# A second feed-forward that begins with two plain chunks in place of four, and the order of ScalarE and VectorE up to there

## The reference

```python
x = x + 0.5 * swiglu_ffn(rms_norm(x, ffn1_norm), ffn1_w_in, ffn1_w_out)
...  # attention and a recurrent branch side by side, then x = x + [A, B] @ w_out_proj
x = x + 0.5 * swiglu_ffn(rms_norm(x, ffn2_norm), ffn2_w_in, ffn2_w_out)

def swiglu_ffn(h, w_in, w_out):          # w_in 1024 x 5632, w_out 2816 x 1024
    g, u = jnp.split(h @ w_in, 2, axis=-1)
    return (jax.nn.silu(g) * u) @ w_out
```

## Time and profile before

| | us |
|---|---|
| median of 3 runs | 896.06 (895.53 to 896.11) |
| the profiled execution | 896.09 |
| its span | 894.3 |
| TensorE busy | 885.5, 5458 matmuls |
| VectorE busy | 670.2 |
| ScalarE busy | 476.7 |
| GpSimd busy | 66.1 |
| mean granted clock of TensorE | 1.00 |

### The profile page before, as it was taken

How to read it: one execution, slowest core, us unless ns; L and a number is a source line. 1 busy time by engine, 2 the same in 40 slices (tenths; PEclk the granted TensorE clock), 3 DMA queues, 4 the chain that set the end, 5 groups by cost and what they waited for, 6 DMA issues and landing times.

```text
span 894.3 us, 14559 instructions
## 1 busy us (share of the span) xinstructions
PE 885.5 (99%) x5458; PEld 788.3 (88%) x5458; DVE 670.2 (75%) x1203; ACT 476.7 (53%) x811; POOL 66.1 (7%) x97
## 2 busy tenths in 40 slices
PE   8999999999999999999999999999999999999998
PEld 7899988999999888888886788899988899999886
DVE  6998864788887567876889787798854788887342
ACT  6766522467665244456657655476621567765120
POOL 0011100112110000000000000011100111210000
PEclk9999999999999999999999999999999999999999
DMA  7366533677775324322221021267633667775340
GB/s 245 127 147 173 146 118 106 166 196 181 183 179 149 107 85 150 101 88 94 95 95 48 1 95 51 99 158 184 158 106 117 165 169 200 178 183 152 106 129 35
DMA packets 26685, 117.70 MB, mean 132 GB/s; under 512 B 3216, under 2 KB 3344, under 8 KB 19344
## 3 DMA queue, kind: packets, MB, share of 16 engines
q1 hardware_dynamic: 16128, 88.32, 28.4%
q0 software_dynamic: 10512, 28.84, 17.6%
HBM read 86.74 MB, written 2.10 MB: 99 GB/s over the span
## 4 chain that ended last, share of the span: by engine, by line
PE 95%; DVE 3%; DMA 1%; ACT 1%; issue 0%; SPq 0%; DVEq 0%; ACTq 0%
PE bank L1482 31%; PE bank L1484 31%; PE bank L1483 30%; PE bank L1709 1%; PE bank L1732 1%; DMA raw<-w_in_dram 1%; DVE w_lo L904 0%; PE bank L1722 0%; DVE small L1403 0%; PE bank L1643 0%; DVE o L1450 0%; ACT probs L855 0%; SPq L418 0%; DVE a_s L1426 0%; DVE x L1393 0%
## 5 line engine op out<-in xcount | busy, mean ns | idle before, releaser
L1482 PE MATMUL bank<-t_hi,w_hi 128*128 128x256 f32 (+1 forms) x848 | 252.5, 298 | 0.6 <-DVE q_part L995 0.5
L1484 PE MATMUL bank<-t_hi,w_lo 128*128 128x256 f32 (+1 forms) x848 | 251.1, 296 | 0.0
L1483 PE MATMUL bank<-t_lo,w_hi 128*128 128x256 f32 (+1 forms) x848 | 250.9, 296 | 0.0
L1482 PEld LDWEIGHTS bank<-t_hi,w_hi 128*128 128x128 f32 x848 | 159.2, 188 | 7.0 <-issue 0.6
L1484 PEld LDWEIGHTS bank<-t_hi,w_lo 128*128 128x128 f32 x848 | 159.3, 188 | 5.3
L1483 PEld LDWEIGHTS bank<-t_lo,w_hi 128*128 128x128 f32 x848 | 158.8, 187 | 5.5
L536 ACT ACTIVATE w_hi<-raw 128x1024 fp32r<-128x1024 f32 (+2 forms) x106 | 89.0, 888 | 129.2 <-PE bank L1484 129.2
L1482 PE MATMUL bank<-act_hi,w_hi 128*128 128x512 f32 x352 | 137.0, 389 | 0.0
L1484 PE MATMUL bank<-act_hi,w_lo 128*128 128x512 f32 x352 | 137.0, 389 | 0.0
L1483 PE MATMUL bank<-act_lo,w_hi 128*128 128x512 f32 x352 | 136.9, 389 | 0.0
L904 DVE TENSOR_TENSOR w_lo<-raw,w_hi 128x1024 fp32r<-128x1024 f32 (+2 forms) x106 | 103.5, 1018 | 9.5 <-ACT w_hi L536 9.0
(11 more groups left out here) (230 smaller groups left out, 1599.9 us busy)
## 6 DMA issues: line engine op xcount, KB each, us to landing
raw<-w_in_dram SPq DMA_DIRECT2D x43, 1024.0 KB, 4.8
w_lo<-raw POOLq DMA_DIRECT2D x36, 512.0 KB, 5.6
w_lo<-raw POOLq DMA_DIRECT2D x36, 256.0 KB, 3.3
raw<-w_out1b_dram SPq DMA_DIRECT2D x8, 768.0 KB, 4.4
raw<-w_qkv_dram SPq DMA_DIRECT2D x6, 1024.0 KB, 4.8
raw<-w_out2b_dram SPq DMA_DIRECT2D x8, 768.0 KB, 4.3
raw<-w_out1a_dram SPq DMA_DIRECT2D x8, 640.0 KB, 3.8
raw<-w_out2a_dram SPq DMA_DIRECT2D x8, 640.0 KB, 3.8
```

Of the source, the lines that this page charges most:

```text
L1482: pe.matmul(dst, s_hi, m_hi, start=first, stop=False, skip_group_check=added)
L1483: pe.matmul(dst, s_hi, m_lo, start=False, stop=False, skip_group_check=added)
L1484: return pe.matmul(dst, s_lo, m_hi, start=False, stop=last, skip_group_check=added)
```

## The change

The second feed-forward has two plain chunks and 20 of seven products (the first group: two plain, eight of seven). Around its start the work of ScalarE and VectorE is written out in one list each (second_start), up to Silu and product of the first chunk of seven; the steps of the general kind begin with chunk c0 + 3. In detail:

- The T combinations of the first two pairs of tiles move up into the loop over the tiles of x, in halves, and those of the other two pairs to the start of the feed-forward.
- The second plain chunk (c0 + 1) gets its low part by the negated copy and two added DMAs of 512 KB each, in halves, in place of VectorE's two lows.
- The plain chunks use other banks of PSUM, and so TensorE's first matmul waits for the fifth updated tile of x.
- The first chunk of seven waits in its third product for the root, and no longer the last plain chunk in its second half.
- A table load for Silu is brought ahead by a tiny activation behind the root.

```diff
-PLAIN = (4, 4)
+PLAIN = (4, 2)
...
+ADDED = (C_IN2 + 1,)
...
-    return 2 * sum(kind(n) != "W" for n in range(c + 1))
+    return 2 * sum(kind(n) != "W" and n not in ADDED for n in range(c + 1))
...
-        SUM_BANKS, COL_BANK = (6, 4, 6), 5
+        SUM_BANKS, COL_BANK = (6, 4, 5), 5
...
-        PLAIN_BANKS = ((0, 1), (3, 4), (2, 7), (5, 6))
+        PLAIN_BANKS = (((0, 1), (3, 4), (2, 7), (5, 6)), ((3, 4), (6, 7)))
...  SyncE, consumed(c)
+                elif c in ADDED:
+                    sp.wait_ge(high_made, 2 * c + 2)
+                    for j in range(2):
+                        sp.wait_ge(added_landed[j], 16 * (ADDED.index(c) + 1))
...  GpSimd, ahead of the first a_lows
+            def added_lows(c):
+                for j in range(2):
+                    pool.wait_ge(added_minus, 2 * ADDED.index(c) + j + 1)
+                    at = c % 2 * SLOT + j * SLOT // 2
+                    pool.dma_start(w_lo[:, at:at + SLOT // 2].bitcast(F32), raw[:, at:at + SLOT // 2],
+                                   accum_op=ALU.add).then_inc(added_landed[j], 16)
...  ScalarE
+            def added_minus_highs(c, parts=range(2)):
+                act.wait_ge(raw_landed[c % 2], 16 * (c // 2 + 1))
+                act.wait_ge(chunk_used, c + 1)
+                for j in parts:
+                    at = c % 2 * SLOT + j * SLOT // 2
+                    act.activation(w_lo[:, at:at + SLOT // 2], raw[:, at:at + SLOT // 2], ACT.Copy, scale=-1.0).then_inc(added_minus, 1)
...  ScalarE, after the square of x tile k
+                if k in (1, 3):
+                    t_bases(1, k // 2)
+                if k in (4, 6):
+                    t_highs(1, k // 2 - 2)
+                if k in (5, 7):
+                    added_minus_highs(C_IN2 + 1, (k // 2 - 2,))
...  ScalarE, ffn(1): sum_highs(3), highs(c0 + 1), t_bases(1, 2), t_bases(1, 3), then
+                    minus_highs(c0 + PLAIN[1])
                     root(3)
-                    highs(c0 + 2, IN_COLS)
-                for c in range(c0, c0 + FFN_CHUNKS):
+                    bring_table(ACT.Silu)
+                    a_highs(c0 + PLAIN[1])
+                    t_highs(f, 2)
+                    t_highs(f, 3)
+                    second_start()
+                for c in range(c0 + 3 * f, c0 + FFN_CHUNKS):
...  ScalarE
+            def second_start():
+                c0, first = C_IN2, C_IN2 + PLAIN[1]
+                s_highs(first, 0, c0)
+                s_highs(first, 2)
+                s_highs(first, 3)
+                s_highs(first, 5, c0 + 1)
+                minus_highs(first + 1)
+                copies(first, 0)
+                copies(first, 1)
+                silu(1, c0)
+                silu(1, c0 + 1)
+                act_highs(1, c0)
+                s_highs(first + 1, 0)
+                act_highs(1, c0 + 1)
+                a_highs(first + 1)
+                for op in S_OPS[1:]:
+                    s_highs(first + 1, op)
+                silu(1, first)
...  VectorE, after x tile k is updated, ahead of its low part
+                if 2 <= k < 6:
+                    t_made_of(1, k // 2 - 1, (k % 2,))
+                if k == 6:
+                    t_lows(1, 0)
...  VectorE, ffn(1): t_lows(1, 1), then
+            def second_start():
+                c0, first = C_IN2, C_IN2 + PLAIN[1]
+                sum_lows(3)
+                s123(first)
+                s4(first)
+                t_made_of(1, 2)
+                t_made_of(1, 3)
+                t_lows(1, 2)
+                t_lows(1, 3)
+                for op in S_OPS[:3]:
+                    s_lows(first, op)
+                reciprocal_root(3)
+                gate(1, c0)
+                s_lows(first, 5)
+                gate(1, c0 + 1)
+                take_q6(first)
+                take_q5(first)
+                product(1, c0)
+                s123(first + 1)
+                act_lows(1, c0)
+                up_earlier(first)
+                product(1, c0 + 1)
...
+                s_lows(first + 1, 3)
+                gate_later(first)
+                gate_earlier(first)
+                s_lows(first + 1, 5)
+                up_later(first)
+                product(1, first)
+                s123(first + 2)
...  TensorE, first_plain
+                    if f == 1 and k == 0:
+                        pe.wait_ge(x_updated, X_UPDATED[1] + 5)
...  TensorE, plain
+                    if c in ADDED:
+                        pe.wait_ge(high_made, 2 * c + j + 1)
+                        pe.wait_ge(added_landed[j], 16 * (ADDED.index(c) + 1))
...
-                if c - C_FFN[f] == PLAIN[f] - 1:
-                    pe.wait_ge(root_made, (1, 3)[f])
+                if c == C_IN1 + PLAIN[0] - 1:
+                    pe.wait_ge(root_made, 1)
...  TensorE, seven_products
-                            pe.wait_ge(prod_made, FT * f + k - 3)
+                            pe.wait_ge(prod_made, FT * f + k - PLAIN[f] + 1 - f)
...
-                        pe.wait_ge(g_scaled, FT * f + k - 1)
+                        if f == 0:
+                            pe.wait_ge(g_scaled, k - 1)
+                        else:
+                            pe.wait_ge(root_made, 3)
```

More of the change, by code:

```diff
@@ L160, in build @@
         small = sb("small", [P, 160])
[L161 removed]
+        spare = sb("spare", [P, 5])
         ones_r = sb("ones_r", [P, P], F32R)
@@ L693, in ffn @@
                     squares(0, EARLY_SQUARES)
+                if f == 1:
+                    sum_highs(3)
                 highs(c0 + 1, IN_COLS)
@@ L932, in _, with t_made_of @@
             LATER, EARLIER = slice(HALF, SEQ), slice(0, HALF)
-            def t_made_of(f, p):
+            def t_made_of(f, p, parts=range(2)):
                 even, odd = tile(x, 2 * p), tile(x, 2 * p + 1)
@@ L938, in t_made_of @@
                 steps = 2 * (KT // 2 * f + p)
[L939 to L947, removed]
+                if 0 in parts:
+                    if p >= 2:
+                        dve.wait_ge(t_low, KT // 2 * f + p - 1)
+                    dve.tensor_tensor(t_block(p, T1), even[:, LATER], even[:, EARLIER], ALU.subtract).then_inc(t_step, 1)
+                    dve.wait_ge(t_base, KT // 2 * f + p + 1)
+                    dve.scalar_tensor_tensor(t_block(p, T3), even[:, EARLIER], g_even, t_block(p, B22), ALU.mult, ALU.subtract)
+                if 1 in parts:
+                    dve.wait_ge(t_step, steps + 1)
+                    dve.scalar_tensor_tensor(t_block(p, T2), t_block(p, T1), g_even, t_block(p, B22), ALU.mult, ALU.add).then_inc(t_step, 1)
+                    dve.wait_ge(t_step, steps + 2)
+                    dve.scalar_tensor_tensor(t_block(p, T4), odd[:, LATER], g_odd, t_block(p, T2), ALU.mult, ALU.subtract).then_inc(t_sums, 1)
             def t_lows(f, p):
@@ L1050, in gate @@
                 dve.tensor_tensor(both(gate_s, c), plain_bank(f, c, 0), rstd[:, :], ALU.mult).then_inc(g_scaled, 1)
+            def second_start():
[20 more added lines that the diff above has]
+                product(1, c0 + 1)
+                s_lows(first + 1, 0)
+                s4(first + 1)
+                act_lows(1, c0 + 1)
+                s_lows(first + 1, 2)
+                s_lows(first + 1, 3)
[5 more added lines that the diff above has]
+                s123(first + 2)
             def plain_step(f, c):
@@ L1215, in ffn @@
                     add_square(k, k % 2)
-                lows(c0 + 1, IN_COLS)
+                if f == 1:
+                    t_lows(f, 1)
+                else:
+                    lows(c0 + 1, IN_COLS)
                 for k in range(EARLY_SQUARES, KT if f == 0 else 0):
@@ L1524, in plain @@
             def plain(f, c, meanwhile=None):
-                pe.wait_ge(low_made, lows_through(c) - 1)
-                in_tile(f, c, 0, range(KT // 2))
-                pe.wait_ge(low_made, lows_through(c))
-                in_tile(f, c, 0, range(KT // 2, KT))
-                if c - C_FFN[f] == PLAIN[f] - 1:
-                    pe.wait_ge(root_made, (1, 3)[f])
+                for j in range(2):
+                    if c in ADDED:
+                        pe.wait_ge(high_made, 2 * c + j + 1)
+                        pe.wait_ge(added_landed[j], 16 * (ADDED.index(c) + 1))
+                    else:
+                        pe.wait_ge(low_made, lows_through(c) + j - 1)
+                    in_tile(f, c, 0, range(j * KT // 2, (j + 1) * KT // 2))
+                if c == C_IN1 + PLAIN[0] - 1:
+                    pe.wait_ge(root_made, 1)
                 if meanwhile:
```

12 lines of the change are left out of this document (7 added, 5 removed).

## The result

| | before | after |
|---|---|---|
| median of 22 runs, us | 895.45 (894.91 to 896.11) | 896.75 (895.90 to 897.32) |
| profiled execution, its span | 896.09, 894.3 | 896.57, 894.7 |
| plain chunks of the second feed-forward | 44.43 | 22.46 |
| its first group of sevens | 59.45 (six chunks) | 82.53 (eight chunks) |
| together: *the stretch* | 103.88 | 104.99 |

The account below looks back on a forecast made before the run. ScalarE and VectorE's 10.06 us ring, not TensorE's 9.89, bounds the group's end. Silu 584.9 + 10.65 + 4 x 10.06 = 635.8, plus 16.85 gives 652.6, 1.0 later: 896.1 + 1.0 = 897.1 us, range 895.0 to 898.2.

Parts of the forecast that it names:

- TensorE's saving: Second feed-forward: two plain chunks of 10.99 us become two of seven products at 9.89, 2.20 us less.
- VectorE's row: Ahead of the first Silu: VectorE waits until 565.4, then works without a hole, up_earlier ending at 579.1.
- the ring: Chunks of seven products: ScalarE and VectorE go round in 10.06 us, TensorE in 9.89, setting the group's end.
- First product of seven at 570.18: Second feed-forward: the first chunk of seven products is due at 570.18 in place of 592.16.
- The added DMA: Second plain chunk's low part: issued at 555.9, landing 561.1 to 562.8, wanted at 561.94; costs nothing or 0.9 us.
- The rival in which the DMA decides: Second plain chunk: added DMA lands late and delays the row; landing of 9 us gives 898.8 us; chance 0.13.
- ScalarE's row: Ahead of the first chunk of seven: from the sum of squares at 555.9 to T high parts at 565.4.
- TensorE's stops: First chunk's seventh product 0.5 us late; second chunk's fourth, fifth and sixth about 1, 0.3 and 0.8.
- Silu of the first chunk: First chunk of seven: Silu at 584.9, 4.3 us after the second chunk starts.
- The first turn: First to second Silu: 10.65 us instead of 10.06, as three sums stand behind the gates and the product.
- The output group: After the first group of sevens: starts 16.85 us after the sixth Silu, at 652.6 against 651.61.
- The first rival: Row up to the first Silu: in time, TensorE decides, output group at 649.8, 894.2 us; chance 0.10.

Follow-up runs that it names:

- e3: Changed kernel with ScalarE's two high parts of the raw weights moved behind the s_highs of the second and third product in every chunk's step: 893.91 us.
- e5: Changed kernel with one extra, unread 512-column sum on VectorE right ahead of the reciprocal: 897.25 us.
- e6: Changed kernel with one extra, unread 512-column sum on VectorE ahead of the T low parts, where VectorE sits idle: 896.79 us.
- e1: Changed kernel with VectorE's three sums for the chunk after next put ahead of the first chunk's gate: 897.97 us.
- e2: Changed kernel with the Silu table load behind ScalarE's three s_highs instead of right behind the root: 896.01 us.
- e7: Changed kernel with a_highs behind two s_highs, in the general steps and in second_start, and the Silu table load behind the three s_highs: 893.86 us.
- e9: The changed kernel again, unedited, on one chip with another version: 896.71 us.

## Why the prediction was right

The forecast was 897.1, and both halves of the argument were seen: TensorE's saving is there, and VectorE's row and the ring behind it give it back, and more: 2.8 of the lost 3.41 are the stops that the row makes in the first two chunks, 0.6 are the ring's. By its own steps:

- **The ring, 10.06 against 9.89.** Right, and shown: the period is read in the rows, and e3 takes it away and gets back the 0.6 that the group's later chunks had lost.
- **First product of seven at 570.18.** 569.51 + 0.68 = 570.19. The tile loop and the wait for the fifth x tile cost TensorE nothing (22.46 for the two plain chunks).
- **The added DMA.** The second was taken as 5.2 from its issue at 555.9, so landing at 561.1 at the earliest. It was issued 0.3 later (555.54 + 0.68) and took 4.9: it landed at 560.43 + 0.68 = 561.11, ahead of the 561.94 at which TensorE wants it. The second plain chunk has 10.99 and no stop. The rival in which the DMA decides is out.
- **ScalarE's row, then VectorE's.** T high parts end at 565.4 in the forecast and at 564.59 + 0.68 = 565.27; VectorE was to wait 1.9 and waited 1.77; up_earlier ends at 579.1 in both (578.42 + 0.68). The table load with the tiny activation behind it has 1.40 of ScalarE's row (560.49 to 561.89), forecast 1.43. e5 and e6 show that this row is the path and that what stands ahead of the wait is not.
- **TensorE's stops.** Forecast 0.5, then 1, 0.3 and 0.8. The gaps beyond 0.12 are 0.48, 0.97, 0.16 and 0.86.
- **Silu of the first chunk.** 584.9 in the forecast, 584.84 in the trace.
- **The first turn** is the term that was mis-sized: 10.65 in the forecast, 10.80 measured. The sentence on its cause was worse than its number. It reads as if the order were a loss; e1 shows the opposite: the stretch is 1.22 longer without it.
- **The output group.** 652.6 in the forecast, 652.72 in the trace.

What the steps did not hold: the place of the next wait. The row was drawn as if only its own length mattered, and TensorE's third product, for which take_q5 waits, was in no step. It did no harm, since VectorE came 0.5 us too late to meet it (take_q5's own instruction starts 27.44 after the first plain matmul in the kernel after, at 574.49, and 26.90 in e2, held by the wait). The first rival, *the row is in time*, would have had to pass it. Two readings were off as well. The longest wait in the table behind the earlier trace rows is not a few tenths but 2.6, for GpSimd at the start of the program; nothing here hangs on it. And 0.2% is too coarse for what can be told apart: with 22 executions of each kernel the interval is 0.05% to either side.

Some of the closeness is luck. The median of before was shown as 896.06 from three runs and is 895.45 from 22. On that base the forecast of +1.0 gives 896.45, 0.3 below the measured 896.75, where the forecast as it stands is 0.35 above. And of the +1.3 the traces have 1.11 in the stretch; the other 0.2 is in no trace and inside the interval, which runs from 0.7 to 1.7 us.

## What to carry to other kernels

Read the pace of a loop from when the same instruction comes round again, engine by engine: TensorE at 99% with hardly a wait can still be only 0.17 us a chunk faster than the ring that feeds it, and then a saving on it counts only if the ring starts earlier too. When work moves up ahead of a short stage, write the following engine's row out to its end, with every wait for TensorE's products in it, the hidden ones too; in e2 the next two in line took back 1.0 of the 1.53 that the edit had won. Ahead of an instruction for which the bounding engine waits, put only what that instruction needs, and let the rest follow it, even if the loop elsewhere has another order (e1); but look for who waits for the rest (in e7 a_highs came 0.7 late).

## What the runs showed of the hardware that was not expected

- A stop costs TensorE somewhat more than the wait. Behind the stop of 0.81 the next matmul starts 0.19 later (585.21 to 585.40), in place of 0.12; behind the 0.32 it is 0.22 (578.48 to 578.70).
- The accumulating DMA of 512 KB took 4.5 and 4.9 us where it goes alone, in the kernel after and again in e9, and 5.2 to 6.9 where each follows a smaller one.
- At a granted clock of 1.00 throughout, matmuls of 256 columns came every 117.7 ns in most of the groups and every 113.4 in a spell of the kernel after (607.85 to 615.79). Such spells lie elsewhere in other executions: in e6 and e2 one shortens a larger group to 118.34, from 118.9. What decides it is open.
